# The projection fillers of the attention stage, cut in two and moved behind the scores

## What is computed

```
proj = x @ w_in[l] + b_in[l]
# forgetting attention, per block of 128 queries, 4 heads of 64:
s = einsum(q[qs:qe], k[:qe]) * scale + c[qs:qe] - c[:qe];  p = softmax(masked s);  o = p @ v[:qe]
# memory attention, 4 heads, 256 memory tokens:
p = softmax(mq @ mk.T * scale);  o = p @ mv
# retention: q, k, v and gate come from 1024 further columns of proj
```

## Time and profile before

| | us |
|---|---|
| median of three runs | 3505.27 |
| the profiled execution, its own time | 3507.59 |
| its span | 3505.9 |
| TensorE busy | 3003.2 (86%) |
| VectorE busy | 1577.7 (45%) |
| ScalarE busy | 1142.4 (33%) |

### The profile page before, as it was taken

How to read it: one execution, slowest core, us unless ns; L and a number is a source line. 1 busy time by engine, 2 the same in 40 slices (tenths; PEclk the granted TensorE clock), 3 DMA queues, 4 the chain that set the end, 5 groups by cost and what they waited for, 6 DMA issues and landing times.

```text
span 3505.9 us, 46865 instructions
## 1 busy us (share of the span) xinstructions
PE 3003.2 (86%) x15514; PEld 1622.2 (46%) x15515; DVE 1577.7 (45%) x2569; ACT 1142.4 (33%) x1781; POOL 260.9 (7%) x162
## 2 busy tenths in 40 slices
PE   6899898999988649999368998989999885699992
PEld 3456554454434425454134665545444343354541
DVE  3333453333234348656533334533433333477656
ACT  3223303222122047556221333032222210467652
POOL 0000000000001240000410000000000023200004
PEclk8989899999999779999678997999999997899995
DMA  9200101101111088777511001011111122689754
GB/s 366 99 1 1 49 1 46 46 31 46 46 54 72 31 323 335 284 273 298 192 60 61 1 1 49 1 46 46 46 37 42 52 79 80 233 334 372 304 227 162
DMA packets 157046, 422.68 MB, mean 121 GB/s; under 512 B 13957, under 2 KB 59185, under 8 KB 156049
## 3 DMA queue, kind: packets, MB, share of 16 engines
q1 hardware_dynamic: 133408, 328.65, 25.6%
q10 hardware_dynamic: 13552, 55.58, 4.0%
q0 software_dynamic: 9920, 36.29, 2.9%
HBM read 352.31 MB, written 72.35 MB: 121 GB/s over the span
## 4 chain that ended last, share of the span: by engine, by line
PE 71%; issue 9%; DVE 7%; DMA 3%; PEld 2%; ACT 2%; POOL 2%; DVEq 1%; POOLq 1%; SPq 1%; PEldq 0%; ACTq 0%
PE PA L1769 14%; PE PA L1429 10%; PE PA L1430 10%; PE PA L1431 10%; PE PB L1788 7%; PE PC L1410 2%; PE PB L1431 2%; PE PB L1429 2%; PE PB L1430 2%; PE PB L1523 1%; DVE W L901 1%; DMA W<-in_w_in_dram 1%; PE PD L1550 1%; POOLq L529 1%; POOL RC L530 1%
## 5 line engine op out<-in xcount | busy, mean ns | idle before, releaser
L1769 PE MATMUL PA<-XT,RA 128*128 128x512 f16 x2304 | 511.2, 382 | 36.7 <-DVE RA L901 33.0
L1429 PE MATMUL PA<-XT,W 128*128 128x512 f16 x1216 | 471.0, 387 | 70.9 <-DVE W L901 70.2
L1431 PE MATMUL PA<-XT,W 128*128 128x512 f16 x1216 | 470.3, 387 | 0.0
L1430 PE MATMUL PA<-XT,W 128*128 128x512 f16 x1216 | 470.1, 387 | 0.0
L1769 PEld LDWEIGHTS PA<-XT,RA 128*128 128x128 f16 x2304 | 226.8, 99 | 303.4 <-issue 42.0
L901 DVE SCALAR_TENSOR_TENSOR XT<-OT,XT 128x1024 f16<-128x1024 f32 x256 | 300.4, 1244 | 105.5 <-ACT XT L792 105.4
L792 ACT ACTIVATE XT<-OT 128x1024 f16<-128x1024 f32 x256 | 247.4, 1043 | 149.7 <-DMA OT<-in_w_e_in_dram 107.8
L720 ACT ACTIVATE WK<-PA,bT 128x512 f32<-128x512 f32 x128 | 88.0, 687 | 622.0 <-PE PA L1431 622.0
L901 DVE SCALAR_TENSOR_TENSOR W<-W 128x512 f16<-128x512 f32 (+2 forms) x320 | 199.4, 660 | 174.0 <-ACT W L601 162.0
L1788 PE MATMUL PB<-W,WK 128*128 128x512 f16 x1152 | 260.1, 383 | 8.6 <-DVE W L901 5.8
L1106 DVE SCALAR_TENSOR_TENSOR MKV<-WK,PB 128x512 f32<-128x512 f32 x96 | 66.0, 687 | 421.8 <-PE PB L1431 421.8
(11 more groups left out here) (304 smaller groups left out, 4146.7 us busy)
## 6 DMA issues: line engine op xcount, KB each, us to landing
OT<-in_w_e_in_dram SPq DMA_DIRECT2D x256, 512.0 KB, 7.6
RA<-in_w_e_out_dram SPq DMA_DIRECT2D x128, 512.0 KB, 6.2
W<-in_w_in_dram SPq DMA_DIRECT2D x104, 512.0 KB, 4.5
RA<-rows SPq DMA_DIRECT2D x50, 512.0 KB, 5.2
rows<-WK ACTq DMA_DIRECT2D x48, 512.0 KB, 5.5
rows<-RA ACTq DMA_DIRECT2D x1, 16384.0 KB, 58.1
W<-in_w_branch_dram SPq DMA_DIRECT2D x32, 256.0 KB, 4.7
W<-in_w_out_dram SPq DMA_DIRECT2D x16, 512.0 KB, 5.3
```

The costliest lines, as they stand in the source:

```text
L1429: mm(dst, lhs(0), rhs(0), start=first, stop=False)
L1430: mm(dst, lhs(0), rhs(1), start=False, stop=False)
L1431: return mm(dst, lhs(1), rhs(0), start=False, stop=last)
L1769: q = mm(PA[:, half, :], ROWS[:, a, k * P:(k + 1) * P], EIS[:, b, k, half * HALF:(half + 1) * HALF], start=k == 0 and a + b == 0, stop=k = ...
```

## The change

In tiles 1 to 6 each filler is cut into two parts of 12 matmuls. The parts stand behind `scores` of units 0, 1 (filler 24 + 2t) and 2, 3 (filler 25 + 2t), ahead of `transpose_p` of the same step. Tile 7 keeps both fillers whole in front of unit 0, and tile 0 has none in the stage. VectorE's evictions move with them: to the head of steps i = 2 and i = 4 in tiles 1 to 6. The bank is waited for at the first part of a filler only, and the semaphore `pj` is raised behind the last.

```diff
@@ VectorE, step n @@
-                        if units[n][1] == 0 and units[n][0] > 0:
-                            t = units[n][0]
-                            if t == NT - 1:
-
-                                v.wait_ge(zero_st, 16)
+                        t, i = units[n]
+                        if t == NT - 1 and i == 0:
+
+                            v.wait_ge(zero_st, 16)
+                        if t > 0 and i == (0 if t == NT - 1 else 2):
                             evict_proj(24 + 2 * t, RN[:, t, 0:HALF], C_RQ)
+                        if t > 0 and i == (0 if t == NT - 1 else 4):
                             evict_proj(25 + 2 * t, RN[:, t, HALF:2 * HALF], C_RQ + HALF)
                         softmax_max(n)
@@ TensorE @@
-                def project(j, n, lhs, rhs):
-                    bank_free(j)
-                    for k in range(KD):
+                def project(j, n, lhs, rhs, part=range(KD)):
+                    if part[0] == 0:
+                        bank_free(j)
+                    for k in part:
                         q = product(PA[:, j % 2, 0:n], lambda i: lhs(k, i), lambda i: rhs(k, i), k == 0, k == KD - 1)
-                    q.then_inc(pj, 1)
+                    if part[-1] == KD - 1:
+                        q.then_inc(pj, 1)
                     return q
...
-                def project_pair(first, t, which, j):
+                def project_pair(first, t, which, j, part=range(KD)):
                     u = first + which
                     if t == 0:
                         unit_loaded(u)
-                    project(j, HALF, lambda k, i: XS[:, i, k, t * P:(t + 1) * P], lambda k, i: WS[u % 2][:, k, i, :])
-                    if t == NT - 1:
+                    project(j, HALF, lambda k, i: XS[:, i, k, t * P:(t + 1) * P], lambda k, i: WS[u % 2][:, k, i, :],
+                            part)
+                    if t == NT - 1 and part[-1] == KD - 1:
                         pe.drain().then_inc(w_used, 1)
@@ TensorE, step n @@
-                        if i == 0 and t > 0:
+                        if t == NT - 1 and i == 0:
                             project_pair(4, t, 0, 24 + 2 * t)
                             project_pair(4, t, 1, 25 + 2 * t)
                         scores(n)
+                        if i < 4 and 0 < t < NT - 1:
+                            project_pair(4, t, i // 2, 24 + 2 * t + i // 2, range(i % 2 * 4, i % 2 * 4 + 4))
```

## The result

The changed kernel takes 3548.56 us (median of four runs, 3545.05 to 3551.68), the kernel before 3505.16 on the same chip: a ratio of 1.0126, 95% interval 1.0109 to 1.0144. That is 43 us slower by the medians, 44 by the ratio; 3544 had been predicted, within 3523 to 3562.

The account below looks back on a forecast made before the run. The prediction took attention to be bound by TensorE's own work. Its terms summed to +19.3 us per layer, +38.6 in two layers, from 3507.6 to 3546.2, less 2.3 for the median: 3544 us, range 3523 to 3562.

Parts of the forecast that it names:

- small waits removed: Inside the tiles, TensorE's short waits for exponentials and the copy of PC go: -4.4 us per layer, bounds -6.0 and -3.1.
- waits, ends of tiles 1 to 5: TensorE stands before the next unit 0's scores, 2.8 us at tile 1 to 1.6 at tile 5: +11 us per layer.
- eviction in front of unit 4's maximum: Moved to step 4's head, it lengthens the chain by 0.2 us each time: +1 us per layer, bounds 0 and 3.5.
- end of tile 0: TensorE idles 3.0 us at the slow clock, whose rise comes later: +4.9 us per layer.
- slow clock, tiles 1 to 5: Behind the new waits, four clock falls per layer, each 3.4 us at half speed: +6.8 us, bounds 0 and 17.
- (C): Tile ends: TensorE's other work covers the wait, only removed waits count: -9 us, 3496 us; chance 0.06.
- (D): Losses at tile ends and gains inside the tiles cancel within 7 us; chance 0.03.
- (A): The new waits are too short to lower the clock: +25 us, 3530 us; chance 0.27.
- (B): The clock stays low 6.8 us behind every new wait, with only the smaller gain: +62 us, 3567 us; chance 0.11.

Follow-up runs that it names:

- waits of tiles 1 to 5 filled: The changed kernel with unused float16 matmuls in front of the first scores of tiles 2 to 6, none at tile 1: 3528.20 us, ratio 1.0070.
- first part in front: The changed kernel with the first 12-matmul part moved in front of unit 0's scores in tiles 1 to 6: 3495.35 us, ratio 0.9976.
- the kernels with filled waits: The changed kernel with unused matmuls in front of the first scores of tiles 1 to 6 (3520.12 us), or of tiles 2 to 6 only (3528.20 us).
- four kernels with dense fillers behind it: The kernel before, or first part in front, with waits for unit 4's exponentials added ahead of fillers: 3526.49, 3539.49, 3538.32 and 3559.83 us.
- the kernel with longer waits: The kernel before plus waits ahead of whole fillers and 12 unused matmuls behind unit 3's scores, tiles 1 to 5: 3559.83 us, 26 us being the added matmuls.

## Why the prediction was right

The sign and the mechanism came from one line of code read against one timeline: scores of unit 0 wait for exponentials that end 4.6 us after the scores of unit 4, and the filler stood in that gap. The traces allow the sum to be taken apart between instructions that all kernels have: the scores of unit 4 of tiles 0, 1 and 6 (us, layer 1 and layer 2).

| kernel | tile 0 to 1 | tile 1 to 6 |
|---|---|---|
| before | 24.41, 23.65 | 139.30, 139.27 |
| changed | 27.44, 27.38 | 158.31, 158.61 |
| waits of tiles 1 to 5 filled | 27.23, 27.60 | 147.37, 147.37 |
| first part in front | 22.76, 23.01 | 136.70, 136.72 |

Term by term, per layer:

| term | predicted | measured | from |
|---|---|---|---|
| small waits removed | -4.4 | -4.2 and -3.2 | first part in front, less before |
| waits, ends of tiles 1 to 5 | +11 | +10.6 | idle time before L1527; waits filled, less first part in front: 10.7 |
| eviction in front of unit 4's maximum | +1 | 0 | the maximum starts 1.18 us behind the scores in both |
| end of tile 0 | +4.9 | +4.7 and +4.4 | tile 0 to 1, changed less first part in front |
| slow clock, tiles 1 to 5 | +6.8 | +10.9 and +11.2 | tile 1 to 6, changed less waits filled |
| sum | 19.3 | 22.0 and 23.1 | changed less before, tile 0 to 6 |

*The removed waits.* I took the middle between two drawings of the same waits (3.1 and 6.0), and the kernel that has this gain alone gives 3.2 to 4.2. The two layers differ in the stretch from tile 0 to 1, where the clock of the kernel before rises 5.2 us behind unit 4's scores in layer 1 and 3.7 in layer 2; from tile 1 to 6 both gain 2.6. I had let all of the waits go; 0.3 us behind each unit 4 stays, as no part covers it.

*The waits at the tile ends.* The first was forecast at 2.8 and shows 2.77; that of tile 5 at 1.6 and shows 1.45; that of tile 0 at 3.0 and shows 2.81.

*The eviction.* I had added the eviction behind the last normalising instruction and got 0.2 us. The trace has `normalize` of unit 1 end at 220.00, the eviction start at 219.93 and end at 220.61, and the maximum start at 220.56: each overlaps the next a little, and there was just room.

*The end of tile 0.* I had chosen between a rise of the clock 3.4 and one 6.8 us later, and took the later. The clock rose at 202.9, but in this trace the stage runs 1.5 us ahead of the kernel before (191.94 against 193.47). Measured from the scores of unit 4 the rise came 11.0 us behind them, against 5.2 before: 5.7 us later, between the two bounds and nearer the one I had taken. The choice rested on a weak argument, so part of this hit is luck.

*The clock.* This is the term that was too small, 6.8 where 11 were measured. I had counted four slow stretches of 3.4 us in each layer, short ones "as the filler part behind it is dense". But the half-height scores stand right behind the wait, ahead of the part. With a part put between wait and scores the stretches do last 3.4 us each. In the changed kernel there are five and four in one trace and five and five in another, and two in each layer or more last 6.8 us. The length, more than the count, is the error: 13.6 us slow were expected, 23.8 came. The eviction's term, 1 us too large, hid a little of it.

Of the rivals, (C), the covered wait, is ruled out by the trace. (D), a sum within 7 us, is ruled out by the time. (A), no fall of the clock, is ruled out by the slow stretches in both traces of the changed kernel and by the kernels with filled waits: (A) gave 3530 for the changed kernel, and 3528 is what it takes with the clock held up by extra work. The rule of the Trainium skill ("TensorE: Matmul & The Clock Gate", "Why this matters for your kernels") about gaps of some 3 us is too lenient for this stage: gaps down to 1.45 us were followed by the slow clock. (B), 6.8 us of slow clock behind every wait, came true behind 9 of the 20 waits in those two traces.

What the kernels on the clock settle, and what they do not. A slow stretch is longer when the scores stand right behind the wait: 6.8 us in 9 of 19 cases, against none of 23 in the four kernels with dense fillers behind it. With the waits filled no slow stretch is left, so the waits bring them. Slow stretches were more frequent in the kernel with longer waits (two of ten, then six of ten, with the same filler behind), but that kernel also has more work ahead of the waits, and length does not decide by itself: 2.85 us brought a slow stretch in one layer and not in the other, and 2.12 us brought none where 1.78 brought one. What decides in the single case stays open. No run shifts the whole stage in time with its waits as they are, so the rival that the moment of the wait matters is untested.

## What to carry to other kernels

A filler in front of an instruction may be covering a wait that no list of waits shows, because the engine does not stand while it is covered. Before moving it, list what the instruction behind it waits for, and measure that chain from the trace: here 4.7 us against 1.9 us of other work. Cut the filler so that one piece stays in the longest gap and the others go to the small ones; that order gave 8 us (0.24%), the change without it cost 44. And price a new wait on TensorE with the clock that it brings down: here the slow stretches cost as much again as the waits.

## What the hardware showed that I had not expected

Adding 56 useless matmuls per layer to the changed kernel made it 28 us faster, because TensorE's granted clock stayed at 1.00. And behind two waits of 2.85 us at the same place of the program, one in each layer, with dense matmuls behind both, the clock fell once and stayed up once.
